# Gate and up of an expert quad in one 512-column product, and no filler matmuls between h and down

## The chip, the cores and the metric

The kernel runs on one core of a Trainium2 chip. The metric is the device time of one execution in microseconds; the median of three runs of the kernel before is 392.3 us.

## What is computed

A decoder block on 256 tokens of width 1024: a gated convolution and block attention in parallel, merged through one output projection and a layer norm, then a mixture of 32 gated experts (four groups of eight; each token takes the best two experts of its best group), and a second layer norm. The change lies in the experts:

```python
g_top_p, g_top = lax.top_k(g_prob, 1)
e_top_logit, e_top = lax.top_k(e_in_group, EXPERT_TOPK)          # two experts of the group
gate = g_top_p * jax.nn.softmax(e_top_logit, axis=-1)
combine = jnp.sum(jax.nn.one_hot(expert_id, N_EXPERTS) * gate[..., None], axis=1)
h = (jax.nn.silu(jnp.einsum('td,edf->tef', xt, w_gate))
     * jnp.einsum('td,edf->tef', xt, w_up)
     * combine[..., None].astype(x.dtype))
ffn = jnp.einsum('tef,efd->td', h, w_down)
```

D_MODEL is 1024, D_EXPERT 256, all float32. An expert has 1 MB each of gate, up and down weights, so the 32 experts have 96 MB.

## The kernel before

The mixer part (to about 190 us) is not touched. Expert work starts with the router at about 185 us. The experts are worked off in eight *quads* of four (`QE` = 4, `NQ` = 8). A round handles one quad for up to 32 tokens of each of its experts (`SLOTS` = 32); with these inputs each quad needs one round, so there are eight rounds. TensorE's columns are split into four groups of 32, one per expert of the quad, so that the matmuls of the four experts run side by side: a *step* below is one such group of four instructions. Each float32 matmul stands in the trace as two instructions, so the matmuls of one chunk for four experts are two steps.

A round on TensorE, in `quad` (L1465):

- `gather` (L1437): 16 matmuls bring the chosen tokens, as eight chunks `xg[:, k, :]` of 128 features, into banks 4, 7 and 5. ScalarE (`take_gathered`, L778, semaphore `xg_a`) writes chunks 0 to 3 to SBUF, VectorE (L1097, `xg_v`) chunks 4 to 7.
- the product (L1494): gate into bank 6 (`part` 0), then up into bank 5 (`part` 1), each 8 chunks x 4 experts, 256 columns wide. Each chunk of the gate half has its own wait. The last instruction of each third of the gate half counts up `gate_ps[i]`, the last of up `gu_ps`.
- transposes of `pick` (L1504), then of `hs` (L1513), then three small matmuls of the identity (`stay_warm(WARM_ROUND[1], 5)`, L1299) which compute nothing that is used, while ScalarE copies hT.
- down (L1530) in three pieces of 512, 256 and 256 columns, into banks 4, 5 and 6 (`Y_PIECES`), and scatter (L1542), which adds the rows to the sums in banks 0 to 3.

On ScalarE `compute` (L781) waits for `gate_ps[-1]`, computes the sigmoid of the gate (L784), then copies hT (L786), put (L790) and ys (L794). On VectorE `compute` (L1120) multiplies sg by the gate (L1123), then by up from bank 5 into hs (L1127), and picks the next quad's slots (L1068). Sigmoid and L1123 need only the gate half and run while up is computed.

Weights come by SyncE's DMA queue, in program order. Two buffers hold gate and up (`gu0`, `gu1`), one holds down (`dn`); quad 1's down weights sit in four early tiles. `load_gu` of quad q waits for `gu_ps` of quad q-2 (L550), `load_dn` of quad q for `y_ps` of quad q-1 (L552, for quad 3 L546). Quad 2's gate loads (L534) wait for quad 0's `gate_ps[i]`. A product of quads 1 to 6 waits for all its gate and up loads (L1473). In quad 7 each expert's gate and up load has its own semaphore (L1479), with 2, 4 and 6 small matmuls between the waits of the up half (L1481), and down comes in pieces by rows and columns (L451).

The end: layer norm 2, partly by matmuls (L1572 to L1583), and four output DMAs.

Of the kernel before, what the change touches and what calls it, by code (L numbers as in the profile page):

```python
# [34 lines left out]
KC = DM // P  # L35
# [3 lines left out]
NG, EPG, DE = 4, 8, 256  # L39
NE = NG * EPG  # L40
FC = DE // P
QE = 4
NQ = NE // QE
SLOTS = P // QE
# [21 lines left out]
WARM_ROUND = 4, 3  # L66
WARM_LAST = 2, 4, 6
WARM_ROUTE = 9
KHALF = KC // 2
KPARTS = ((0, 2), (2, KHALF), (KHALF, KC))  # L70
XG_BANK = 4, 7, 5
GATE_PARTS = KPARTS
# [3 lines left out]
def hybrid_block(nc, x, w_in, conv_w, w_out_conv, w_out_attn, w_o, ln1_g, ln1_b,  # L76
# [18 lines left out]
    with ctx:  # L95
# [546 lines left out]
        def _(act):  # L642
# [137 lines left out]

            def compute(n):  # L781

                act.wait_ge(gate_ps[-1], n)
                act.activation(sg[:, :], bank[6][:, 0:DE], ACT.Sigmoid).then_inc(sg_done, 1)  # L784
                act.wait_ge(hT_ps, n)
                act.activation(hT[:, :, :], bank[4][:, 0:SEQ].rearrange("p (j s) -> p j s", j=FC),  # L786
                               ACT.Copy).then_inc(hT_done, 1)
                act.wait_ge(put_ps, n)
                act.wait_ge(bank_free[6], n + 1)
                act.activation(put[:, :], bank[7][:, SEQ:2 * SEQ], ACT.Copy).then_inc(put_done, 1)  # L790
                for i in (0, 2):
                    b, lo, hi = Y_PIECES[i]
                    act.wait_ge(y_ps, NY * n - (NY - 1) + i)
                    act.activation(ys[:, lo:hi], bank[b][:, 0:hi - lo], ACT.Copy).then_inc(y_taken[i], 1)  # L794
# [27 lines left out]
        def _(dve):  # L822
# [297 lines left out]
            def compute(c, coming):  # L1120

                dve.wait_ge(sg_done, c + 1)
                dve.tensor_tensor(sg[:, :], sg[:, :], bank[6][:, 0:DE],  # L1123
                                  ALU.mult).then_inc(round_link, 1)
                dve.wait_ge(round_link, 2 * c + 2)
                dve.wait_ge(gu_ps, c + 1)
                dve.tensor_tensor(hs[:, :], sg[:, :], bank[5][:, 0:DE],  # L1127
                                  ALU.mult).then_inc(bank_free[6], 1)
                dve.wait_ge(put_ps, c + 1)
                pick_slots(coming)  # L1130
# [58 lines left out]
        def _(pe):  # L1189
# [275 lines left out]
            def quad(q, first, half, loads, last_quad):  # L1465

                    w = gu[half]
                    end = pe.alloc_register(f"end{q}")
                    with pe.Fori(first, end) as c:
                        gather(c, range(NK - 1 if q == 0 else NK))  # L1470
                        pe.wait_ge(bank_free[6], c + 1)
                        if not last_quad:
                            pe.wait_ge(gu_in[half], 16 * QE * (2 * loads - (half == 0 and loads > 1)))  # L1473
                        if q == 2:
                            pe.wait_ge(gate2_in, 16 * len(GATE_PARTS))
                        for part in range(2):
                            if last_quad:
                                for e in range(QE):
                                    pe.wait_ge(last_gu_in[part][e], 16)  # L1479
                                    if part and e < QE - 1:  # L1480
                                        stay_warm(WARM_LAST[e])  # L1481
                            for k in range(KC):
                                if last_quad and part == 1 and k == KHALF:
                                    pe.wait_ge(last_up_end, 16)
                                if q == 0 and part == 0 and k == KHALF:
                                    pe.wait_ge(rank_read, 1)
                                    gather(c, [NK - 1])
                                if part == 0 and k < KC // 2:
                                    pe.wait_ge(xg_a, KC // 2 * c + k + 1)
                                elif part == 0:  # L1490
                                    pe.wait_ge(xg_v, KC // 2 * c + k - KC // 2 + 1)
                                for e in range(QE):
                                    g = slice(SLOTS * e, SLOTS * (e + 1))
                                    mm = pe.matmul(bank[6 - part][g, 0:DE], xg[:, k, g],  # L1494
                                                   w[:, e, part, k, :],
                                                   start=(k == 0), stop=(k == KC - 1), skip_group_check=True)
                                for i, (_, hi) in enumerate(GATE_PARTS):
                                    if part == 0 and k == hi - 1:
                                        mm.then_inc(gate_ps[i], 1)
                            if part == 1:  # L1500
                                mm.then_inc(gu_ps, 1)
                        pe.wait_ge(pickw_done, 2 * c + 2)
                        for t in range(TT):
                            mm = pe.transpose(bank[7][:, SEQ + t * P:SEQ + (t + 1) * P],  # L1504
                                              pick[:, t, :, :].rearrange("p e s -> p (e s)"), ident[:, :])
                        mm.then_inc(put_ps, 1)
                        if q == 0:
                            pe.wait_ge(rounds_done, 1)
                        upto = pe.value_load(bounds[0:1, q + 1:q + 2], min_val=1, max_val=MAX_ROUNDS)
                        pe.reg_mov(end, upto)  # L1510
                        pe.wait_ge(bank_free[6], c + 2)
                        for j in range(FC):
                            mm = pe.transpose(bank[4][:, j * P:(j + 1) * P], hs[:, j::FC],  # L1513
                                              ident[:, :])
                        mm.then_inc(hT_ps, 1)
                        stay_warm(WARM_ROUND[1], 5)
                        pe.wait_ge(hT_done, c + 1)
                        def down(i, rows=range(FC)):

                            b, lo, hi = Y_PIECES[i]  # L1520
                            if last_quad and i == 0:
                                pe.wait_ge(dn_left_in[rows[0]], 16)
                            elif last_quad:
                                pe.wait_ge(dn_cols_in[i] if FC - 1 in rows else dn_first_rows_in, 16)
                            elif i == 0:
                                dn_loaded(q)
                            for j in rows:
                                for e in range(QE):
                                    g = slice(SLOTS * e, SLOTS * (e + 1))
                                    mm = pe.matmul(bank[b][g, 0:hi - lo], hT[:, j, g], dn_of(q, e)[:, j, lo:hi],  # L1530
                                                   start=(j == 0), stop=(j == FC - 1), skip_group_check=True)
                            if FC - 1 in rows:
                                mm.then_inc(y_ps, 1)

                        def scatter(i, tiles=range(TT)):

                            _, lo, hi = Y_PIECES[i]
                            pe.wait_ge(y_taken[i], c + 1)
                            if i == 0:
                                pe.wait_ge(put_done, c + 1)  # L1540
                            for t in tiles:
                                pe.matmul(bank[2 * t + lo // HALF][:, lo % HALF:lo % HALF + hi - lo],  # L1542
                                          put[:, t * P:(t + 1) * P], ys[:, lo:hi], start=False, stop=True,
                                          skip_group_check=True).then_inc(added, 1)

                        if last_quad:
                            down(0, [0])
                            down(0, [1])
                            scatter(0)
                            down(1, [0])  # L1550
                            down(2, [0])
                            down(1, [1])
                            down(2, [1])
                            for t in range(TT):
                                scatter(1, [t])
                                scatter(2, [t])
                        else:
                            for i in range(NY):
                                down(i)
                            for i in range(NY):  # L1560
                                scatter(i)
                    return pe.snap(end, min_val=1, max_val=MAX_ROUNDS)
# [45 lines left out]
```

## Time and profile before

| what | value |
|---|---|
| runs | 392.15, 392.3, 394.7 us; median 392.3 |
| profiled execution | 392.49 us |
| its span, first to last instruction | 390.2 us |
| TensorE matmuls busy | 358.6 us, 92% |
| VectorE, ScalarE, GpSimd busy | 161.3, 138.0, 35.2 us |
| mean granted TensorE clock | 0.974 of 2.4 GHz |
| moved by DMA | 132.79 MB, mean 340 GB/s |
| L1494 (gate and up), matmuls | 1024 instructions, 61.8 us busy |

How to read it: the profile is one execution. Busy time of an engine is the union of its instructions; weight loads (PEld) overlap matmuls (PE). "SPq" is SyncE issuing a DMA. A transfer's landing is told as microseconds from its issue. In a timeline row the bracket gives the engine's idle time before it and who ended it. The granted clock is 1.00 at 2.4 GHz and 0.50 at 1.2 GHz.

### The profile page before, as it was taken

How to read it: one execution, taken by the hardware profiler on the slowest of the kernel's cores; microseconds unless marked ns; L12 is line 12 of the kernel's file. 1: busy time of each engine (PE TensorE's matmuls, PEld its weight loads, DVE VectorE, ACT ScalarE, POOL GpSimd, SP SyncE). 2: the span in 40 equal slices, each digit the busy share in tenths (PEclk: the TensorE clock that was granted, in tenths of full speed). 3: DMA queues.
4: the chain of work that ended last, by engine and by line, in shares of the span. 5: the costliest groups of instructions: out<-in, count | busy, mean ns of one | idle time of the engine just before them, and what ended most of it. 6: DMA issues, size and time to landing. Idle time of an engine off the chain costs nothing.

```text
span 390.2 us, 8014 instructions
## 1 busy us (share of the span) xinstructions
PE 358.6 (92%) x3331; PEld 284.4 (73%) x3331; DVE 161.3 (41%) x337; ACT 138.0 (35%) x240; POOL 35.2 (9%) x42
## 2 busy tenths in 40 slices
PE   7999999999999999999899999999599398299995
PEld 7999988999999999998657575656256156157642
DVE  3546579797465656464730303030610111010235
ACT  4643565655535444435723131322112113012012
POOL 3310000000000000001000005207711000000001
PEclk9999999999999999999999999999899699599999
DMA  8699884966759889799899999999999999999962
GB/s 281 204 329 373 302 280 160 349 221 217 269 180 306 279 264 376 228 392 375 306 365 429 425 422 427 425 419 423 426 423 413 427 427 427 427 426 425 412 245 108
DMA packets 52053, 132.79 MB, mean 340 GB/s; under 512 B 2818, under 2 KB 36626, under 8 KB 41012
## 3 DMA queue, kind: packets, MB, share of 16 engines
q1 hardware_dynamic: 51572, 131.88, 87.7%
q8 instruction: 26, 0.43, 0.4%
q0 software_dynamic: 304, 0.17, 0.2%
q10 hardware_dynamic: 144, 0.26, 0.2%
q14 instruction: 7, 0.06, 0.0%
HBM read 131.25 MB, written 1.05 MB: 339 GB/s over the span
## 4 chain that ended last, share of the span: by engine, by line
PE 67%; DMA 16%; SPq 8%; DVE 5%; ACT 2%; issue 1%; DVEq 0%; ACTq 0%
PE bank L1200 15%; DMA gu<-in_w_up 14%; PE bank L1494 10%; PE bank L1229 8%; PE bank L1362 6%; PE bank L1530 6%; PE bank L1232 4%; PE bank L1445 4%; PE bank L1542 4%; SPq L469 4%; SPq L434 3%; PE bank L1344 3%; PE bank L1299 2%; DMA raw<-in_w_in 2%; DVE wl L835 2%
## 5 line engine op out<-in xcount | busy, mean ns | idle before, releaser
L835 DVE TENSOR_TENSOR wl<-raw,wh 128x1024 fp32r<-128x1024 f32 x54 | 65.8, 1223 | 55.0 <-ACT wh L653 54.8
L1494 PE MATMUL bank<-gu,xg 128*32 128x256 f32 x1024 | 61.8, 401 | 20.4 <-DMA gu<-in_w_up 19.8
L653 ACT ACTIVATE wh<-raw 128x1024 fp32r<-128x1024 f32 x54 | 56.5, 1056 | 59.8 <-DMA raw<-in_w_in 20.2
L1494 PEld LDWEIGHTS bank<-gu,xg 128*32 128x32 f32 x1024 | 33.4, 116 | 45.4 <-issue 25.0
L1229 PE MATMUL bank<-xh,wh 128*128 128x256 f32 x176 | 44.1, 288 | 0.5 <-ACT qT L715 0.5
L1229 PE MATMUL bank<-xl,wh 128*128 128x256 f32 x176 | 43.1, 283 | 0.0
L1229 PEld LDWEIGHTS bank<-xh,wh 128*128 128x128 f32 x176 | 33.6, 191 | 2.7 <-issue 2.0
L1097 DVE TENSOR_SCALAR xg<-bank,gcol,bcol 128x128 f32<-128x128 f32 x32 | 10.9, 404 | 59.0 <-PE bank L1445 59.0
L1229 PEld LDWEIGHTS bank<-xl,wh 128*128 128x128 f32 x176 | 33.7, 191 | 0.0
L1445 PEld LDWEIGHTS bank<-pick,x1p 128*128 128x128 f32 x256 | 29.8, 192 | 1.9 <-issue 0.9
L1445 PE MATMUL bank<-pick,x1p 128*128 128x128 f32 x256 | 30.2, 276 | 0.6 <-DVE pick L1068 0.6
L1542 PE MATMUL bank<-ys,put 128*128 128x256 f32 (+1 forms) x96 | 30.0, 461 | 0.7 <-ACT ys L794 0.7
L1542 PEld LDWEIGHTS bank<-ys,put 128*128 128x128 f32 x96 | 17.4, 189 | 13.6 <-issue 10.1
L1200 PE MATMUL bank<-xh,wl 128*128 128x256 f32 x96 | 27.2, 283 | 0.0
L1200 PE MATMUL bank<-xl,wh 128*128 128x256 f32 x96 | 27.2, 283 | 0.0
L1200 PE MATMUL bank<-xh,wh 128*128 128x256 f32 x96 | 27.2, 283 | 0.0
L1530 PE MATMUL bank<-dn,hT 128*32 128x256 f32 (+1 forms) x324 | 25.9, 453 | 0.0
L778 ACT ACTIVATE xg<-bank,bcol,gcol 128x128 f32<-128x128 f32 x32 | 12.9, 454 | 34.0 <-PE bank L1445 33.4
L1232 PE MATMUL bank<-xh,wl 128*128 128x256 f32 x176 | 24.7, 283 | 0.0
L1232 PEld LDWEIGHTS bank<-xh,wl 128*128 128x128 f32 x176 | 22.7, 192 | 0.0
L784 ACT ACTIVATE sg<-bank 128x256 f32<-128x256 f32 x8 | 3.1, 383 | 48.9 <-PE bank L1494 48.9
L1123 DVE TENSOR_TENSOR sg<-sg,bank 128x256 f32<-128x256 f32 x8 | 3.4, 422 | 37.5 <-ACT sg L784 37.5
(234 smaller groups left out, 588.7 us busy)
## 6 DMA issues: line engine op xcount, KB each, us to landing
gu<-in_w_up SPq DMA_DIRECT2D x31, 1024.0 KB, 19.6
gu<-in_w_gate SPq DMA_DIRECT2D x30, 1024.0 KB, 15.0
dn<-in_w_down SPq DMA_DIRECT2D x26, 1024.0 KB, 17.6
raw<-in_w_in SPq DMA_DIRECT2D x40, 512.0 KB, 5.6
raw<-in_w_o SPq DMA_DIRECT2D x8, 512.0 KB, 5.0
raw<-in_w_out_conv SPq DMA_DIRECT2D x4, 512.0 KB, 4.0
raw<-in_w_out_attn SPq DMA_DIRECT2D x4, 512.0 KB, 5.0
gu<-in_w_gate SPq DMA_DIRECT2D x1, 2048.0 KB, 10.7
```

Source lines behind the costliest of these rows:

```text
L469: sp.dma_start(gu[(NQ - 1) % 2][:, e, c, ks, :], (wg_v, wu_v)[c][:, (NQ - 1) * QE + e, ks, :]).then_inc(last_up_end if i else last_gu_in[c ...
L653: act.activation(wh[:, s, :].rearrange("p (k c) -> p k c", k=KC), raw[pair % NRAW][:, :].rearrange("p (k c) -> p k c", k=KC) [:, :, n % 2 ...
L778: act.activation(xg[:, k, :], bank[XG_BANK[i]][:, (k - lo) * P:(k - lo + 1) * P], ACT.Identity, scale=gcol[:, k:k + 1], bias=bcol[:, k:k + ...
L835: dve.tensor_tensor(wl[:, s, :].rearrange("p (k c) -> p k c", k=KC), raw[pair % NRAW][:, :].rearrange("p (k c) -> p k c", k=KC) [:, :, n % ...
L1200: mm = pe.matmul(dst, w[:, k, :], v[:, i, :], start=(i == 0 and w is h and v is high_in), stop=(i == len(ks) - 1 and w is l))
L1229: pe.matmul(dst, h[:, k, :], v[:, k, :], start=(k == 0 and v is xh), stop=False)
L1232: mm = pe.matmul(dst, l[:, k, :], xh[:, k, :], start=False, stop=(k == KC - 1))
L1362: mm = pe.matmul(bank[2 * t + h][:, :], v[:, m, t * P:(t + 1) * P], w[:, s, h * HALF:(h + 1) * HALF], start=(j == 0 and m == 0 and i == 0) ...
L1445: mm = pe.matmul(bank[XG_BANK[i]][:, (k - lo) * P:(k - lo + 1) * P], x1p[:, t, k, :], pick[:, t, :, :].rearrange("p e s -> p (e s)"), star ...
L1494: mm = pe.matmul(bank[6 - part][g, 0:DE], xg[:, k, g], w[:, e, part, k, :], start=(k == 0), stop=(k == KC - 1), skip_group_check=True)
L1530: mm = pe.matmul(bank[b][g, 0:hi - lo], hT[:, j, g], dn_of(q, e)[:, j, lo:hi], start=(j == 0), stop=(j == FC - 1), skip_group_check=True)
L1542: pe.matmul(bank[2 * t + lo // HALF][:, lo % HALF:lo % HALF + hi - lo], put[:, t * P:(t + 1) * P], ys[:, lo:hi], start=False, stop=True, s ...
```

## The change

Three things change, all in the expert rounds.

1. In quads 1 to 6 (the second to seventh) gate and up become one product: for each chunk and expert one matmul moves 512 columns, gate and up side by side, into bank 6. Waits for the gathered chunks stand once per third, not per chunk. Quads 0 and 7 keep two halves of 256 columns, but up goes to columns 256 to 511 of bank 6, no longer to bank 5.
2. ScalarE's sigmoid waits for the end of the whole product (`gu_ps`) instead of the end of the gate half, in all quads, and VectorE reads up from bank 6.
3. The three small matmuls between the transposes of hs and down remain in the last quad only.

```diff
             def compute(n):
-                act.wait_ge(gate_ps[-1], n)
+                act.wait_ge(gu_ps, n)
                 act.activation(sg[:, :], bank[6][:, 0:DE], ACT.Sigmoid).then_inc(sg_done, 1)
...
                 dve.wait_ge(gu_ps, c + 1)
-                dve.tensor_tensor(hs[:, :], sg[:, :], bank[5][:, 0:DE],
+                dve.tensor_tensor(hs[:, :], sg[:, :], bank[6][:, DE:2 * DE],
                                   ALU.mult).then_inc(bank_free[6], 1)
...
-                        for part in range(2):
-                            if last_quad:
+                        def gathered(k):
+                            if k < KC // 2:
+                                pe.wait_ge(xg_a, KC // 2 * c + k + 1)
+                            else:
+                                pe.wait_ge(xg_v, KC // 2 * c + k - KC // 2 + 1)
+                        def project(k, parts):
+                            for e in range(QE):
+                                g = slice(SLOTS * e, SLOTS * (e + 1))
+                                mm = pe.matmul(bank[6][g, parts.start * DE:parts.stop * DE], xg[:, k, g],
+                                               w[:, e, parts, k, :],
+                                               start=(k == 0), stop=(k == KC - 1), skip_group_check=True)
+                            return mm
+                        if 0 < q < NQ - 1:
+                            for lo, hi in GATE_PARTS:
+                                gathered(hi - 1)
+                                for k in range(lo, hi):
+                                    mm = project(k, slice(0, 2))
+                            mm.then_inc(gu_ps, 1)
+                        elif q == 0:
+                            for i, (lo, hi) in enumerate(GATE_PARTS):
+                                if hi == KC:
+                                    pe.wait_ge(rank_read, 1)
+                                    gather(c, [NK - 1])
+                                for k in range(lo, hi):
+                                    gathered(k)
+                                    mm = project(k, slice(0, 1))
+                                mm.then_inc(gate_ps[i], 1)
+                            for k in range(KC):
+                                mm = project(k, slice(1, 2))
+                            mm.then_inc(gu_ps, 1)
+                        else:
+                            for part in range(2):
                                 for e in range(QE):
                                     pe.wait_ge(last_gu_in[part][e], 16)
                                     if part and e < QE - 1:
                                         stay_warm(WARM_LAST[e])
...
+                                for k in range(KC):
+                                    if part and k == KHALF:
+                                        pe.wait_ge(last_up_end, 16)
+                                    if not part:
+                                        gathered(k)
+                                    mm = project(k, slice(part, part + 1))
+                            mm.then_inc(gu_ps, 1)
...
                         mm.then_inc(hT_ps, 1)
-                        stay_warm(WARM_ROUND[1], 5)
+                        if last_quad:
+                            stay_warm(WARM_ROUND[1], 5)
                         pe.wait_ge(hT_done, c + 1)
```

The DMA issues, their order and the events that they wait for stay as they were.

## Rows read from the trace of the kernel before

**Rows 1.** The page, GB/s in 40 equal slices of 9.76 us.
```profile
GB/s 281 204 329 373 302 280 160 349 221 217 269 180 306 279 264 376 228 392 375 306 365 429 425 422 427 425 419 423 426 423 413 427 427 427 427 426 425 412 245 108
```

**Rows 2.** Windows: from:to, length; busy PE, PEld, DVE, ACT, POOL; clock; DMA share, GB/s.
```profile
186.00:192.00 6.00, 4.97 (x42) 4.30 (x43) 4.75 (x30) 4.88 (x5) 0.00 (x0) 1.00 0.94 286
211.40:231.00 19.60, 19.35 (x232) 12.60 (x232) 3.58 (x12) 4.92 (x10) 0.00 (x0) 1.00 1.01 426
...
278.72:281.43 2.71, 2.71 (x28) 1.37 (x32) 1.06 (x1) 0.00 (x0) 2.24 (x3) 0.50 1.01 426
...
330.50:339.06 8.56, 0.00 (x0) 0.00 (x0) 1.85 (x7) 0.34 (x1) 0.00 (x0) 0.62 1.01 429
339.07:342.87 3.80, 3.80 (x36) 1.82 (x40) 0.00 (x0) 0.00 (x0) 0.00 (x0) 0.50 1.01 429
```

**Rows 3.** Chain that ended last, in order of time: start, us, what.
```profile
339.61 26.18 DMA gu<-in_w_up
...
365.83 1.60 PE bank L1299 x12
```

**Rows 4.** Timeline of TensorE in quad 1's down: start, us, engine, line, instruction.
```profile
223.72 0.62 PE L1530 MATMUL bank<-dn_z,hT 128*32 128x512 f32 x1
...
225.04 0.59 PE L1530 MATMUL bank<-dn_z,hT 128*32 128x512 f32 x1
...
225.47 0.38 PE L1530 MATMUL bank<-dn_z,hT 128*32 128x256 f32 x1
...
226.98 0.38 PE L1530 MATMUL bank<-dn_z,hT 128*32 128x256 f32 x1
```

**Rows 5.** Timeline of all engines, quad 1, from the gathered chunks to hT.
```profile
214.03 1.28 ACT L784 ACT_TABLE_LOAD   x1
...
214.89 7.11 PE L1494 MATMUL bank<-gu,xg 128*32 128x256 f32 x128
215.00 1.37 DVE L1097 TENSOR_SCALAR xg<-bank,gcol,bcol 128x128 f32<-128x128 f32 x4 [7.62 <-PE bank L1445]
...
218.62 0.38 ACT L784 ACTIVATE sg<-bank 128x256 f32<-128x256 f32 x1 [3.30 <-PE bank L1494]
219.03 0.42 DVE L1123 TENSOR_TENSOR sg<-sg,bank 128x256 f32<-128x256 f32 x1 [2.18 <-ACT sg L784]
...
222.14 0.42 DVE L1127 TENSOR_TENSOR hs<-sg,bank 128x256 f32<-128x256 f32 x1 [2.69 <-PE bank L1494]
...
223.16 0.38 ACT L786 ACTIVATE hT<-bank 128x256 f32<-128x256 f32 x1 [4.16 <-PE bank L1513]
```

**Rows 6.** Timeline of all engines in quad 7.
```profile
364.14 3.30 PE L1299 MATMUL bank<-ident 128*128 128x128 f32 x24
...
367.37 3.66 PE L1494 MATMUL bank<-gu,xg 128*32 128x256 f32 x64
...
374.74 0.60 ACT L794 ACTIVATE ys<-bank 128x512 f32<-128x512 f32 x1 [1.90 <-PE bank L1530]
...
375.39 1.98 PE L1542 MATMUL bank<-ys,put 128*128 128x512 f32 x4 [0.72 <-ACT ys L794]
...
377.31 2.06 PE L1530 MATMUL bank<-dn,hT 128*32 128x256 f32 x32
378.73 0.16 PEld L1530 LDWEIGHTS bank<-dn,hT 128*32 128x32 f32 x8 [0.40 <-DMA dn<-in_w_down]
```

**Rows 7.** Timeline of SyncE's DMA issues around quad 2's down.
```profile
229.87 0.43 SPq L545 DMA_DIRECT2D dn_r<-in_w_down  x1
247.06 1.35 SPq L443 DMA_DIRECT2D dn<-in_w_down  x3
```

**Rows 8.** DMA issues of the whole span: count, KB each, median us to landing.
```profile
dn_x<-in_w_down SPq DMA_DIRECT2D x1, 1024.0 KB, 4.8
...
dn_r<-in_w_down SPq DMA_DIRECT2D x1, 1024.0 KB, 21.5
```

**Rows 9.** Timeline of TensorE at the start of quad 4's product.
```profile
278.72 8.43 PE L1494 MATMUL bank<-gu,xg 128*32 128x256 f32 x128 [4.88 <-DMA gu<-in_w_up]
```

More of the change, by code:

```diff
@@ L1481, in quad @@
                                         stay_warm(WARM_LAST[e])
[L1482 to L1501, printed above, removed]
+                                for k in range(KC):
[5 more added lines that the diff above has]
+                            mm.then_inc(gu_ps, 1)
                         pe.wait_ge(pickw_done, 2 * c + 2)
```

## The prediction, made before the change was built

> **What bounds the kernel now.** I read the page first, then windows, the chain of waits, and the timeline of one quad and of the tail. The page gives TensorE 92% of the span, which suggests a kernel bound by matmuls. Its strip of DMA rates says otherwise for the part that the change touches: from the slice that begins near 205 us the core moves 412 to 429 GB/s in every slice until the last weights [rows 1]. The windows give the split. In quad 1 TensorE is busy for 19.35 of 19.60 us, while the twelve loads of 1 MB of a quad take 29.5 us at 426 GB/s; the early quads live on weights loaded ahead. Later TensorE runs out of them: before quad 6 it has 8.56 us without a matmul [rows 2]. So the weight stream sets the time, and TensorE counts in two places: where it frees a buffer too late for the queue to stay full, and behind the last weights.
>
> The chain of waits ends in that second place: a load of up weights issued at 339.61 lands 26.18 us later, at 365.79; after it come TensorE's last sums and the layer norm, to 390.2 [rows 3]. It is the third expert's load of quad 7. What reaches the instruction behind it is a run without a hole that began with quad 6's product at 339.07: product, down, scatter, gather, quad 7's gate, then six small warm products (`WARM_LAST` 2 and 4) from 364.14. The six after the wait take 1.54 us (365.83 to the product at 367.37), so the first six end near 365.68, against 365.83: TensorE has 0.15 us of slack there, although it idled 8.56 us before quad 6 [rows 2, 3, 6].
>
> **Part 1, the merged product (quads 1 to 6).** Half of the matmuls and weight loads of L1494 go: 64 products of 256 columns become 32 of 512 per quad. The columns stay. The down product shows both widths in the same layout: a step of 512 columns (four experts side by side) takes 0.43 us (225.04 to 225.47), one of 256 takes 0.2157 on average (225.47 to 226.98 in seven) [rows 4]. A product holds 16 of the first or 32 of the second: 6.88 against 6.90 us, 0.02 gained. At most it is 0.23, if the 7.11 us that L1494 takes in quad 1 fell to 6.88 [rows 5]. The saved weight loads give nothing, since they lie under the matmuls (PEld 12.60 us beside PE 19.35) [rows 2].
>
> **Part 2, fewer gather waits.** In quad 1 ScalarE has done its four pieces of xg when its table load starts at 214.03, before the product at 214.89; VectorE's four end at 216.37, while chunk 4 comes 8 steps of 512 columns, 3.4 us, after the product's start [rows 5]. Every wait is over when it is asked: 0 gained, and 0 lost by coarser waits; without that cover it would be at most VectorE's 1.37.
>
> **Part 3, the sigmoid moves behind the up half (all eight quads).** ScalarE now waits for the end of the whole product, in quads 0 and 7 too, since they share `compute`. Before, sigmoid (L784) and sg times gate (L1123) ran at 218.62 and 219.03, under the up half; only hs (L1127) was exposed. Sigmoid began 0.28 us after the gate's last step (214.89 + 16 x 0.2157 = 218.34), hs 0.35 after the last up step (221.79). Now: 0.28, then 0.41 from sigmoid to L1123, its 0.42, and a hand-over of 0.04 as after other instructions (0.41 less ScalarE's 0.38 is 0.03), so hs begins at 1.15 instead of 0.35: 0.80 us later, in every quad [rows 4, 5]. At most 0.87, if VectorE's slower reaction stays. The table load (1.28 us) precedes the wait and stays under the product [rows 5]. Behind hs VectorE has the next quad's picks, which move with it; the gather wants them 8 us later. The Trainium skill, page "PSUM — Partial Sum Buffer", section "PSUM bank collisions raise a hardware error", says that two engines must not touch one bank and quadrant at once; by it the wait can't be relaxed while gate and up share a bank. No run here shows that.
>
> **Part 4, no small products between h and down (quads 0 to 6).** hT is done at 223.16 + 0.38 = 223.54; from ScalarE to TensorE a hand-over takes 0.05 in the tail (375.34 to 375.39), so down could start at 223.59 instead of 223.72 [rows 4 to 6]. 0.12 gained (0 to 0.13); the products filled a wait for ScalarE.
>
> Per quad 0 to 6: +0.80 - 0.12 - 0.02 = +0.66 us (0.44 to 0.87).
>
> **Does the stream notice?** The thin place is the issue of quad 3's down weights at 247.06, which waits for quad 2's down. The load before it in the queue, issued at 229.87, landed 21.5 later, at 251.4, so 4.3 us of work were queued [rows 7, 8]. Three quads later by 0.66 take 2.0 of it and leave 2.3 (1.7 at the upper bound). The nearest row for a 1 MB load on a lightly filled queue is dn_x, 4.8 us to landing [rows 8]; 2.46 are its bytes at 426 GB/s, 2.3 are not: just covered. I take 0, bounds 0 and 0.7.
> The page "DMA: Bandwidth & Descriptors" of the Trainium skill, in the section on what a DMA costs, gives a fixed part of about 2.0 us, mostly after the last byte; by it the loss is 0 even with a cover of 2.0, and the sum is the same.
>
> Before quad 4 TensorE idles 4.88 us [rows 9]; four shifts (2.6 us) fit in. Its half-clock stretch of 2.71 us [rows 2] may vanish with the shorter idle time, which helps nobody, as quad 5 waits for weights again. Quads 5 and 6 start when weights land, so nothing piles up past them.
>
> **The end.** Quad 6 starts at 339.07 as before; its run comes out 0.66 later, less the slack of 0.15: 0.51. Quad 7's own sigmoid and L1123, no longer under the load of up weights: 0.80 (it keeps its small products and the shape of its product). Against that: eight steps of down from 377.31 should take 1.73 plus some 0.16 of the last one's tail (0.379 less 0.2157), and took 2.06, for a wait for the last down rows before 378.73 [rows 4, 6]. With TensorE later this wait of 0.17 is gone. Sum: 0.51 + 0.80 - 0.17 = **+1.14 us**. The profiled execution took 392.49, 390.2 of it span and 2.3 around it; the sum makes 393.6. It stood 0.2 above the median of 392.3, so against the median the forecast is **393.5 us**.
>
> **The rivals.**
> *Hidden in part by the clock (2 in 10).* Quad 6 begins at 1.2 GHz after its idle time, and 3.80 us of it run so, against 2.71 in quad 4 [rows 2]. If the clock rises as early as there, its run gains (3.80 - 2.71) / 2 = 0.55 and the 0.51 is swallowed by the wait for up weights: 0.80 - 0.17 = +0.63, 392.9 us. For it: one of two rows. Against: the median of the kernel before lies within 0.2 of this execution, so 3.80 isn't odd.
> *A gap in the stream (1 in 10).* If the cover at 247 is short by 0.7, all later landings move: +1.8, 394.1 us. For it: the cover ends as thin as dn_x wants it. Against: it needs the upper bound in all three quads.
> *The clock falls in quads 0 to 2 (slower, 6 in 100).* TensorE's hole grows from 0.35 + 0.6 to about 1.6 us a quad. If the clock fell to 1.2 GHz there for 3.80 us as in quad 6, each fall would cost 1.9. One is just covered by the 2.3 us of queued work; with one in each quad the stream stands still for 5.7 - 2.3 = 3.4, and the time is +1.1 + 3.4 = +4.5, 396.8 us. It decides the sign from the third fall on. Against it: in 186 to 192, with 1.03 of 6 us idle, the clock stays at 1.00 [rows 2].
> *TensorE bounds the quads after all, and shorter code helps (faster, 3 in 100).* Even the 0.23 of part 1 and the 0.13 of part 4 with sigmoid hidden end at the same landing at 365.79: 0.15 before it, 392.2 us. Over 1% only if the loads themselves ran faster, for which nothing speaks.
> The forecast itself holds 6 in 10.
>
> **Numbers.** Forecast 393.5. Range 392.5 to 395.2: below, the case with the clock (392.9) less the scatter of the runs; above, the gap (394.1) with 0.87 in place of 0.66 and 0.80 (0.3) and a clock in quad 6 that rises 1.6 us later (0.8). About 1% (3.9 us) is what a measurement of this kernel can tell from no change. Within it 0.91, slower 0.06, faster 0.03.
>
> **What would show it.** L1494's successor in quads 1 to 6: 32 products of 512 columns in about 7.1 us, as long as before. The start of hs 1.15 us after the last step in all quads, and a period of 20.3 instead of 19.6 us in quads 1 to 3. Quad 6's product at 339.1 and the landing of the third up load at 365.8, each within 0.5; the last up product 0.5 later, the rest of the tail 1.1 later. I am wrong if the period doesn't grow, if the rate falls near 250, if the clock dips before 270, or if quad 6's landing moves.

## The result

The changed kernel takes 394.6 us (median of 20 runs), the kernel before 392.4 (20 runs). The ratio is 1.0054, with a 95% interval of 1.0041 to 1.0067: 2.1 us slower (1.6 to 2.6). The forecast was 393.5 us, +1.2. The sign and the costs in quads 6 and 7 were right. The stream term was not: 0.9 of the 2.1 us lie in a term that I had set to zero.

The profiled execution of the changed kernel spans 391.9 us, against 390.2. One quad of it, in the timeline of all engines (columns as in [rows 5]):

```profile
215.01 1.28 ACT L784 ACT_TABLE_LOAD   x1
215.86 7.07 PE L1487 MATMUL bank<-gu,xg 128*32 128x512 f32 x64
...
223.00 0.38 ACT L784 ACTIVATE sg<-bank 128x256 f32<-128x256 f32 x1 [6.71 <-PE bank L1487]
223.42 0.42 DVE L1123 TENSOR_TENSOR sg<-sg,bank 128x256 f32<-128x256 f32 x1 [5.59 <-ACT sg L784]
223.88 0.42 DVE L1127 TENSOR_TENSOR hs<-sg,bank 128x256 f32<-128x256 f32 x1
...
224.35 0.51 PE L1534 MATMUL bank<-ident,hs 128*128 128x128 f32 x2 [1.05 <-DVE hs L1127]
224.90 0.38 ACT L786 ACTIVATE hT<-bank 128x256 f32<-128x256 f32 x1 [1.51 <-PE bank L1534]
...
225.33 0.62 PE L1552 MATMUL bank<-dn_z,hT 128*32 128x512 f32 x1 [0.47 <-ACT hT L786]
```

The product has half the instructions and the same length, 7.07 us against 7.11. Sigmoid, its product with the gate and hs now run one after the other behind the product. Apart from the transposes of `pick`, TensorE stands idle meanwhile: 1.05 us before the transposes of hs, and 0.47 more until hT is there. Hs starts 8.02 us after the product's start, where it started 7.25 after it [rows 5]; down starts 9.47 after it instead of 8.83 [rows 4, 5]: 0.64 us per quad, forecast 0.66.

Two windows of the changed kernel (columns as in [rows 2]). The first shows what the forecast did not have, the second quad 6's stretch at 1.2 GHz, 3.88 us, which was 3.80 before:

```profile
246.00:254.00 8.00, 8.00 (x72) 4.96 (x65) 0.42 (x1) 1.17 (x3) 2.48 (x2) 1.00 0.93 375
339.69:343.57 3.88, 3.88 (x20) 1.01 (x24) 0.00 (x0) 0.00 (x0) 0.00 (x0) 0.50 1.01 429
```

Over 246 to 254 us the kernel before moves this:

```profile
246.00:254.00 8.00, 8.00 (x64) 6.25 (x56) 0.42 (x1) 2.71 (x6) 2.48 (x2) 1.00 1.01 422
```

375 against 422 GB/s over 8 us is 0.89 us of transfer that did not happen, in a kernel whose end hangs on that stream. It is not made up later: from 254 to 340 us the two kernels move 424 and 423 GB/s.

The tail of the changed kernel, from the chain of waits in 360 to 382 us (start, us, what):

```profile
365.52 2.88 PE bank L1299 x24
368.40 3.63 PE bank L1487 x64
...
372.06 0.39 ACT sg L784
...
372.47 0.43 DVE sg L1123
...
372.93 0.43 DVE hs L1127
...
379.13 1.48 PE bank L1552 x24
...
380.63 0.43 DVE ys L1136
...
381.11 0.91 PE bank L1564 x3
```

The twelve small products run on without a stop: the weights are there before TensorE is. In the kernel before they took 3.23 us from 364.14 to 367.37 with the wait in between [rows 6], here 2.88, so the slack was 0.35 us in that execution.

### The profile page after: what moved, and what is told of

The parts are those of the page before. It is cut to its first block, busy times and chain, and to the rows that moved or that the text cites. A ratio compares the mean times of both kernels' runs of the same rounds, so it can differ in the third digit from the quotient of the medians.

```text
span 391.9 us, 7150 instructions
## 1 busy us (share of the span) xinstructions
PE 354.3 (90%) x2905; PEld 266.4 (68%) x2905; DVE 163.8 (42%) x337; ACT 137.9 (35%) x240; POOL 35.6 (9%) x42
## 3 DMA queue, kind: packets, MB, share of 16 engines
HBM read 131.25 MB, written 1.05 MB: 338 GB/s over the span
## 4 chain that ended last, share of the span: by engine, by line
PE 67%; DMA 17%; DVE 6%; SPq 5%; ACT 3%; issue 1%; DVEq 0%; ACTq 0%
PE bank L1200 15%; DMA gu<-in_w_up 13%; PE bank L1487 12%; PE bank L1229 8%; PE bank L1552 6%; PE bank L1362 6%; PE bank L1232 4%; SPq L434 4%; PE bank L1445 4%; PE bank L1564 4%; DMA raw<-in_w_in 3%; PE bank L1344 3%; DVE wl L835 2%; ACT wh L653 1%; PE bank L1299 1%
## 5 line engine op out<-in xcount | busy, mean ns | idle before, releaser
L1487 PE MATMUL bank<-gu,xg 128*32 128x512 f32 (+1 forms) x640 | 61.7, 540 | 14.8 <-DMA gu<-in_w_up 14.2
L1487 PEld LDWEIGHTS bank<-gu,xg 128*32 128x32 f32 x640 | 20.5, 115 | 50.1 <-issue 43.8
L1552 PE MATMUL bank<-dn,hT 128*32 128x256 f32 (+1 forms) x324 | 27.5, 475 | 2.6 <-ACT hT L786 1.9
```

Source lines behind the costliest of these rows:

```text
L1487: mm = pe.matmul(bank[6][g, parts.start * DE:parts.stop * DE], xg[:, k, g], w[:, e, parts, k, :], start=(k == 0), stop=(k == KC - 1), skip ...
```

## The experiments

"Before" is the kernel before, whose runs on the same chip go with each group. Each ratio is to it.

**The late sigmoid, by place.** The kernel before with only this, in all quads, in 0 to 2, in 3 to 6, or in 7 (for the partial ones ScalarE's loop is cut in two, or the last call differs):

```diff
             def compute(n):
-                act.wait_ge(gate_ps[-1], n)
+                act.wait_ge(gu_ps, n)
```

> The kernel before with one edit: ScalarE's sigmoid waits for the end of the whole product in all eight quads; gate and up stay two halves in banks 6 and 5, the small products stay. Theory A (the late sigmoid is all of the change's loss, in three places: quads 0 to 2 by way of the stream, quad 6's run, quad 7's tail): hs 0.80 us later in each quad, quad period 20.4 us, quad 3's down weights issued 2.4 us later than in the kernel before, all weight landings after about 250 us later by 0.7 to 1.5, the end 2.1 to 2.9 us later, ratio 1.005 to 1.007. Rival B (the 512-column products or the up half in bank 6 cost the time): 0 to +0.3 us here, ratio below 1.001.

Measured: 1.0058 (1.0039 to 1.0076), 394.9 us. With the products of 256 columns, up in bank 5 and all small products in place, the late sigmoid alone is as slow as the whole change. Rival B falls.

> The kernel before with the sigmoid late in quads 0 to 2 only. Theory A1 (three late quads leave too little queued work at the issue of quad 3's down weights, and the stream has a gap that it never gets back): landings after 252 us later by 0.7 to 1.5 us, end +0.7 to +1.5 us, ratio 1.002 to 1.004. Rival A2 (the queued work still covers it, as the prediction put it; the loss of 1.3 us seen there in the changed kernel was chance): period 20.4 in quads 0 to 2, but landings within 0.3, end 0 to +0.3 us, ratio below 1.001.

Measured: 1.0036 (1.0014 to 1.0058), +1.4 us, with quad 7 as before. Its window shows the gap, so A2 falls:

```profile
246.00:254.00 8.00, 8.00 (x70) 5.72 (x63) 0.42 (x1) 2.23 (x6) 2.48 (x2) 1.00 0.92 355
```

> The kernel before with the sigmoid late in quads 3 to 6 only. Theory A1: quads 3 to 5 are followed by idle time of TensorE and cost nothing, quad 6 costs 0.80 less the slack of 0.35 before the last up product: +0.45 us, ratio 1.001. Rival (every late quad costs the same wherever it stands, 2.1 / 8 each): +1.05 us, ratio 1.0027.

Measured: 1.0018 (0.9999 to 1.0037), +0.7 us, and no gap at 246 to 254 (417 GB/s). Both theories lie in the interval; the number alone doesn't decide between 0.45 and 1.05. Nor does the profile: quad 6's product took 8.38 us in it against 8.97 in the kernel before, because the clock rose after 2.6 us of it instead of 3.8. Over the fourteen profiled executions this product takes 8.4 to 9.9 us, a scatter as large as the costs that are sought here.

> The kernel before with the sigmoid late in quad 7 only. Theory A: hs of quad 7 at 0.80 us later against the end of its product, and the end +0.80 us, ratio 1.002; TensorE's 0.14 to 0.17 us wait for the last down rows doesn't give anything back, since the next product waits for VectorE's copy. The prediction's term: +0.63 us, ratio 1.0016. Rival: the last down rows land late enough to hide it: 0.

Measured: 1.0014 (0.9993 to 1.0036), +0.55 us; the interval holds 0. The profile is sharper than the time: from the start of the last up product (367.07) to the end of the span are 23.6 us, against 22.8 in the kernel before, 0.8 more. Timeline of its tail:

```profile
370.80 0.38 ACT L784 ACTIVATE sg<-bank 128x256 f32<-128x256 f32 x1 [11.68 <-PE bank L1494]
371.22 0.42 DVE L1123 TENSOR_TENSOR sg<-sg,bank 128x256 f32<-128x256 f32 x1 [9.26 <-ACT sg L784]
371.67 0.42 DVE L1127 TENSOR_TENSOR hs<-sg,bank 128x256 f32<-128x256 f32 x1
...
377.81 1.93 PE L1530 MATMUL bank<-dn,hT 128*32 128x256 f32 x32
379.38 0.42 DVE L1136 COPY ys<-bank 128x256 f32<-128x256 f32 x1 [1.62 <-PE bank L1530]
...
379.86 1.99 PE L1542 MATMUL bank<-ys,put 128*128 128x256 f32 x8
```

The last two pieces of down (eight steps) now run in 1.93 us, without the wait for the last rows (2.06 before, [rows 6]), and still L1542 starts 2.05 us after 377.81, exactly as long after down's start as in the kernel before. It waits for VectorE's copy (L1136) of the piece of down that is complete earlier. The 0.17 us that the forecast took back were never on the path. The three partial kernels add up to 2.7 us, against 2.3 for late_all, which their intervals allow.

**The thin place in the queue.** Two of quad 4's gate loads go ahead of quad 3's down loads:

```diff
+            sp.wait_ge(gu_ps, through(3))
+            load_gu(0, 4, [0, 1], parts=[0])
             sp.wait_ge(y_ps, NY * through(3))
             for e in range(1, QE):
                 load_dn_one(3, e)
             for q in range(4, NQ - 1):
                 sp.wait_ge(gu_ps, through(q - 1))
-                load_gu(q % 2, q)
+                if q == 4:
+                    load_gu(0, 4, [2, 3], parts=[0])
+                    load_gu(0, 4, parts=[1])
+                else:
+                    load_gu(q % 2, q)
```

> The changed kernel, with two of quad 4's gate loads issued as soon as quad 2's product is done, ahead of quad 3's down loads instead of behind them (2 MB, 4.9 us more work in the queue at the thin place). Theory A (the late sigmoid drains the queue there and costs 0.9 us of stream): the rate in 246 to 254 us back at about 422 GB/s from 375, all later landings 0.9 us earlier than in the changed kernel, ratio to the kernel before 1.0031 instead of 1.0054. Rival A2 (the thin place is chance or is made up later): ratio unchanged, 1.005. Rival A3 (quad 3's down rows land too late behind the two loads): TensorE waits before quad 3's down, the queue thins out later instead.

Measured: 0.9999 (0.9980 to 1.0018), 392.6 us: all of the loss gone, more than expected, and 425 GB/s in the window:

```profile
246.00:254.00 8.00, 7.53 (x64) 4.05 (x64) 0.49 (x2) 1.64 (x4) 2.48 (x2) 1.00 1.01 425
```

> The kernel before with the same move of two gate loads. Theory A (there the queue is never empty, 422 GB/s in 246 to 254): no change, ratio 0.999 to 1.001. Rival (the move helps whatever the sigmoid does): ratio 0.998 or less.

Measured: 0.9969 (0.9956 to 0.9981), 391.5 us. Here theory A is wrong: the move helps the kernel before as well, although its profile shows no gap to close. Of the 2.2 us that the changed kernel gained by it (1.0054 to 0.9999), some 1.2 would thus not be the gap of the change, if the move gives both kernels the same. Against before_gate_ahead the changed kernel with the move is still 0.0030 or 1.2 us slower.

> The changed kernel with the two gate loads ahead, and with quad 7 as in the kernel before: its gate in bank 6, up in bank 5, its sigmoid after the gate half. What stays of the change are the merged products and the late sigmoid in quads 0 to 6. Theory A: both the stream's 0.9 and the tail's 0.80 are gone, quad 6's 0.66 less 0.35 of slack stays: +0.3 us, ratio 1.0008. Rival (something else in the changed kernel costs the rest, such as up in bank 6 in quad 0): ratio 1.002 or more.

Measured: 0.9970 (0.9953 to 0.9987), 391.4 us. That is the merged product and the late sigmoid in quads 0 to 6, at no cost against before_gate_ahead (0.9969) that can be seen; the intervals are 0.5 and 0.7 us wide to either side, so the expected 0.3 us of quad 6 may be there. From after_gate_ahead to here, quad 7's part of the change, are 0.0029 or 1.1 us, where 0.80 was expected. The expected 1.0008 lacked what the move gives to the kernel before as well.

> The changed kernel with the three small products between h and down back in all quads. It differs from late_all by the merged product alone (and the bank of up), and from the changed kernel by the small products alone. Theory: the merge gives 0.02 to 0.04 us per quad and the small products cost 0.12, so down starts 0.12 later in quads 0 to 6: queue 0.4 us thinner at the thin place, +0.4 there and +0.1 before quad 7, ratio 1.006 to 1.007, quad period 20.4 us. Rival (the small products keep the clock up and their removal costs): the granted clock differs from the changed kernel's 0.973 by more than 0.003, ratio below 1.0054.

Measured: 1.0052 (1.0029 to 1.0075), 395.0 us, against 1.0054 without the small products and 1.0058 for late_all, which differs by the unmerged product (and the bank of up). Merging is worth nothing that can be seen here, and so are the small products in sum. The expected 1.006 to 1.007 was a bit high; on the clock see below.

**Order or program?** In the three kernels with the move SyncE's last output landed faster, so I put the same instructions in the old order:

```diff
             sp.wait_ge(y_ps, NY * through(3))
             for e in range(1, QE):
                 load_dn_one(3, e)
+            sp.wait_ge(gu_ps, through(3))
+            load_gu(0, 4, [0, 1], parts=[0])
             for q in range(4, NQ - 1):
                 sp.wait_ge(gu_ps, through(q - 1))
```

> The kernel before with SyncE's program written as in before_gate_ahead (the same instructions, one more wait and one more value load), but the two gate loads of quad 4 left behind quad 3's down loads, in the old order. It tells the move of the loads from the mere change of the program. Seen so far: in the three kernels with that program the last output DMA issued by SyncE lands 2.65 us after its issue, in the others 3.3. Theory L (the program's place in memory or length does that): 2.65 us here too, the end 0.65 us earlier, ratio 0.998 to 0.9985. Rival (the order of the loads does it): 3.3 us, ratio 1.000.

Measured: 1.0003 (0.9983 to 1.0022). What SyncE's output line takes to landing (min/median/max of three) is in the kernel before and then in this one:

```profile
DMA to landing us min/median/max: 2.1/2.5/3.3
```

```profile
DMA to landing us min/median/max: 2.0/2.1/2.7
```

So the mere rewriting does shorten the last landing, from 3.3 to 2.7, but the time does not follow clearly: the interval holds 0 and, at its edge, -0.65 us. The gain of 1.2 us in before_gate_ahead thus seems to be at least in part the order's: its interval (to 0.9981) ends where this one's begins.

> The changed kernel with the same rewriting, the loads in the old order. Theory A with L: the rate in 246 to 254 us as low as in the changed kernel (375 GB/s; below 400), the last output 2.65 us after its issue, ratio 1.0054 - 0.0017 = 1.0037; the distance to after_gate_ahead (0.9999) is then what the queue loses at the thin place, 0.9 to 1.6 us. Rival (the late sigmoid costs nothing in the stream, and after_gate_ahead gained by its program alone): ratio 1.000.

Measured: 1.0038 (1.0017 to 1.0058), 394.1 us. The rival (1.000) falls. From here to after_gate_ahead, same instructions and another order, are 0.0039 or 1.5 us. Its profiled execution has the deepest gap of all:

```profile
205.00:210.00 5.00, 5.00 (x46) 1.94 (x39) 0.42 (x1) 0.98 (x2) 0.00 (x0) 0.72 1.04 433
246.00:254.00 8.00, 7.73 (x66) 4.45 (x67) 0.42 (x1) 1.47 (x4) 2.48 (x2) 1.00 0.64 247
```

The first row tells why: the granted clock fell in quad 0's down, which took 1.69 us longer, and the delay below is 1.69 us more than the changed kernel's. Taken by single microseconds, the queue moved 131, 57, 66 and 106 GB/s from 248 to 252 us and 426 from there on. Two of these rows:

```profile
249.00:250.00 1.00, 1.00 (x21) 0.42 (x11) 0.42 (x1) 0.02 (x1) 0.00 (x0) 1.00 0.14 57
252.00:253.00 1.00, 1.00 (x7) 0.87 (x6) 0.00 (x0) 0.00 (x0) 1.00 (x1) 1.00 1.01 426
```

The load before quad 3's down loads in the queue, issued at 232.15, landed 19.0 us later, at 251.15. So the stream had thinned out some 3 us before that load's landing, and it was full again only 2.0 us after the issue at 249.98. Put together, from each kernel's SyncE and TensorE timelines and its window 246 to 254 (delay: issue of quad 3's down loads after the second start of quad 0's product, less the 50.08 us of the kernel before; lost: 8 us x (422 - rate) / 422):

| kernel | delay us | GB/s | lost us |
|---|---|---|---|
| no_fillers | -0.39 | 423 | 0 |
| before, late_last, before_same_code | 0.00, 0.00, -0.01 | 422, 426, 421 | 0 |
| late_3_to_6 | 0.01 | 417 | 0.1 |
| changed kernel | 1.93 | 375 | 0.9 |
| after_with_fillers | 2.31 | 317 | 2.0 |
| late_0_to_2 | 2.38 | 355 | 1.3 |
| late_all | 2.39 | 339 | 1.6 |
| after_same_code | 3.62 | 247 | 3.3 |

The issue that the delay is read from is in [rows 7] for the kernel before, and in after_same_code it is:

```profile
249.98 1.28 SPq L443 DMA_DIRECT2D dn<-in_w_down  x3
```

Roughly, every microsecond of delay beyond the first costs a microsecond of stream. The delay that the queue covered (delay less lost) was 0.3 to 1.1 us in these five executions. The prediction had let it cover 2.0: 4.3 us of queued work less the 2.3 that it took a load to need.

**The small products alone.** The kernel before without them in quads 0 to 6.

```diff
-                        stay_warm(WARM_ROUND[1], 5)
+                        if last_quad:
+                            stay_warm(WARM_ROUND[1], 5)
```

> The kernel before without the three small products between h and down in quads 0 to 6, and nothing else of the change. Theory: down 0.12 us earlier per quad, 0.4 us more work queued at the thin place and 0.12 us more slack before the last up product, worth nothing in the time: ratio 0.999 to 1.0005, clock within 0.966 to 0.976 as before. Rival (they keep the clock at 2.4 GHz): the clock dips before 270 us and the ratio is above 1.001.

Measured: 0.9998 (0.9981 to 1.0016), clock 0.967 to 0.974, and a granted clock of 1.00 up to 270 us in the profiled execution. As expected.

**A faster kernel.** The kernel before with the gate loads ahead, no `stay_warm` between h and down, and:

```diff
-WARM_LAST = 2, 4, 6
+WARM_LAST = 2, 4, 4
```

> A version meant to beat both: the kernel before with two gate loads ahead, none of the small products between h and down, and four instead of six small products after the third up load of quad 7. Theory: those after the third up load end 0.51 us earlier, so the last up product starts when the first half of the fourth load lands, 0.3 us earlier than in before_gate_ahead, and down of quad 7 starts 0.12 earlier: ratio 0.9969 - 0.001 = 0.996. Rival (the clock falls in the tail for want of them): ratio above 0.998.

Measured: 0.9974 (0.9956 to 0.9993), 391.6 us. It beats both kernels, but so does before_gate_ahead (0.9969) without the trimming; the hoped-for 0.3 us is not seen. In its profiled execution the ten small products of quad 7 run without a stop until 366.66 and are themselves what the last up product waits for.

## Why the prediction was right or wrong

**Right, and shown.** *The sigmoid behind the up half is the cost* [rows 5]: late_all reproduces the loss by that one edit. *The weight stream bounds the expert part* [rows 1]: TensorE waits for up weights before quads 4, 5 and 6 in the changed kernel too (3.27, 2.06 and 8.86 us). *0.80 us per hs*: from the last up product's start to hs are 4.60 us (368.33, 372.93) in the changed kernel against 3.80 (367.37, 371.17) before, 0.80. *The merged product gives next to nothing*: 7.07 against 7.11 us in quad 1, and late_all against after_with_fillers. *Gather waits 0*: VectorE's chunks are done at 217.34 in quad 1, before the product comes to them, and the product has no hole. *Quads 3 to 5 absorbed*: before quad 6 TensorE still idles 8.86 us, and its product starts at 339.69 instead of 339.07.

```profile
339.69 8.98 PE L1487 MATMUL bank<-gu,xg 128*32 128x512 f32 x64 [8.86 <-DMA gu<-in_w_up]
```

**Wrong: "Does the stream notice? I take 0."** The step that failed is how long the queue still has work at the issue of quad 3's down loads. I had counted it from the issue to the landing of the load before (4.3 us), taken off 2.0 for three late quads, and held the rest, 2.3, against the 2.3 that dn_x took beyond its bytes [rows 7, 8]: "just covered". The landing is the wrong end to count to. In the changed kernel the load before was issued at 231.48 and landed 21.4 us later, at 252.88; quad 3's loads were issued at 249.30, 3.6 us earlier, and yet in 249 to 251 the queue moved only 238 GB/s, and 377 in 251 to 252. The first of those loads took 6.0 us to land (at 255.30), not 4.8. So the case that I gave 1 in 10 was the one that came, and it didn't need the upper bound in all three quads: the delay was 1.93 us, as forecast. Of the prediction's own signs of being wrong two appeared, the rate near 250 us and quad 6's product, 0.62 us later where 0.5 was allowed. The other price that it set beside dn_x's, by which a cover of 2.0 us loses nothing, gave 0 as well and fails with it. The gap costs 0.9 us in the profiled execution. For the runs as a whole the distance from after_same_code to after_gate_ahead, 1.5 us, is an upper estimate, since in the kernel before the order gained too.

**Mis-sized: the slack before the last up product.** 0.35 us in the profiled execution of the kernel before, not 0.15. I had taken the time of twelve warm instructions from the six products after the wait (1.54 us), which holds the start after a wait; the run without a wait takes 2.88 for twice as many, not 3.08.

**Wrong: the 0.17 us back from the last down rows.** They were off the path, as late_last shows: the scatter waits for VectorE's copy. It was luck that this error (0.17 too little) and that of the slack (0.20 too much) nearly cancel.

**Didn't come: the loss hidden in part by the clock (2 in 10).** In the changed kernel quad 6 ran at 1.2 GHz for 3.88 us, as long as before (3.80), and nothing of the 0.51 was hidden. The size of this term is chance in any one execution, as the 8.4 to 9.9 us of quad 6's product show.

The sum with the measured terms, for the profiled execution: quad 6's product 0.62 later by the stream, + 0.69 over quad 6 (down at 351.07 against 349.76, +1.31), - 0.35 of slack gives 0.96, which is the distance of the last up products (368.33 to 367.37); + 0.80 gives 1.76 at hs; the end is 1.7 later. The stream's 0.62 is less than the 0.89 lost at 250 us; single executions differ by some tenths elsewhere on the way, but I have not traced the rest. With the whole gap in place of 0.62 and the forecast 0.66 the sum is 0.9 + 0.66 - 0.35 + 0.80 = 2.0, against 2.1 measured by the runs; its terms still come from single executions.

**The rival with the clock** was held at 6 in 100, with a fall in each of quads 0 to 2. It is real, in a smaller form. There are four profiled executions of kernels that have the late sigmoid and lack the small products. In each of them the clock fell to 1.2 GHz for a part of down in one or two quads, and down took 5.3 us instead of 3.65: after_same_code in quads 0 and 4, after_gate_ahead in 0 and 5, after_both in 0, and the changed kernel in 4. In the other ten, with only one of the two edits or neither, no quad's down does so. The changed kernel and after_same_code:

```profile
292.20 5.35 PE L1552 MATMUL bank<-dn,hT 128*32 128x512 f32 x48 [0.47 <-ACT hT L786]
204.05 5.34 PE L1558 MATMUL bank<-dn,hT 128*32 128x512 f32 x48 [0.47 <-ACT hT L792]
```

What TensorE did before is in the profile: 1.05 us idle before the transposes of hs, 0.47 before down. But the changed kernel has the same idle times in quads 0 to 2 and a clock of 1.00 there, so they alone don't decide it. A fall in quad 4 or 5 costs nothing here, since TensorE waits for weights afterwards (2.06 us before quad 5 in the changed kernel). A fall in quad 0 lands on the thin place: after_same_code's single one, 1.7 us, came with 3.3 us lost instead of 0.9. The prediction had called one fall "just covered by the 2.3 us of queued work"; those 2.3 it had already spent on the load's own delay.

So "the products filled a wait for ScalarE, 0.12 gained" holds for the wait before the change (no_fillers: quad 3's down loads issued 0.39 us earlier after three quads, no dip of the clock before 270 us); with the longer idle time of the change they also went with a clock that stayed up (late_all, late_0_to_2, after_with_fillers). In the time nothing is seen of either (1.0052 against 1.0054). How many runs of the changed kernel have a fall in quad 0 is open: its mean clock doesn't tell, for after_gate_ahead's execution with two falls has 0.977, and a third of the runs of the kernel before lie at 0.966 to 0.970.

The fourth rival, a faster kernel (3 in 100), fell with the sign of the result.

**Left open:** why the two gate loads ahead make the kernel before 1.2 us faster. The profiled executions with early quads as before show 417 to 426 GB/s in 246 to 254 in either order. That of before_gate_ahead is ahead already before the moved loads can act (313 against 311 GB/s from 0 to 246 us, roughly 1 us of transfer), so it explains nothing. It may be a gap that only some executions have, and in part the faster last output.

## What to carry to other kernels

Where a stream of loads sets the time, work out for each issue that waits for compute how long the queue still has work. Don't count to the landing of the last queued load: here the rate fell some 3 us before that landing, and a new load brought it back 2 us after its issue (both in after_same_code). In this kernel 1.9 us of TensorE time in three early quads, 140 us before the end, cost 0.9 us of stream. Merging two products into one, and so waiting for both before the first one's epilogue, takes away an overlap of 0.80 us per quad here, and with the columns unchanged it gives nothing back (7.07 against 7.11 us). When slack is spent, a cure can be cheap: two loads issued ahead of the wait brought the changed kernel back to the time of the kernel before. That is not the same as no loss, for the kernel before gained 1.2 us by them too.

## What the runs showed of the hardware

The slowest of SyncE's three output DMAs landed 2.7 us after its issue in all six kernels with one more wait and value load in the middle of SyncE's program, whatever the order of the loads. In six of the eight with the old SyncE program it took 3.2 to 3.4 us, in late_3_to_6 3.1 and in late_all 4.7. I have no cause for it, and the time did not clearly follow. But a change of one engine's program is not neutral even where its work stays, and a control with the same instructions is worth a run.

TensorE's clock fell to 1.2 GHz after idle times of 1.05 and 0.47 us between the product and down, in quad 0, 4 or 5 of the four kernels without small products there and with the late sigmoid. It did so in some quads and not in others with the same idle times. [rows 2] (1.03 us idle of 6, clock 1.00) had made me hold it for unlikely.

A stream of 1 MB loads on one queue thinned out before its last load had landed: to 131 GB/s in 248 to 249 us and 57 in 249 to 250, with the landing at 251.15 (after_same_code).
